# A transformer kernel that works out the second norm's sum of squares from sums taken with the output tiles

## The chip, the cores and the metric

One core of one Trainium2 chip runs the whole program. The time is device time in microseconds (us) from launch to end; the median of 3 runs of the kernel before is 2362.94 us (2359.41 to 2363.81).

## The reference

Two layers on 512 tokens of x and 256 tokens of ctx, 1024 channels (ctx is not needed after the first layer's feed-forward part), then one layer of another kind (dilated and neighbourhood attention, a router and experts), which starts with a norm as well. What matters here is how two norms follow one another. Cut to that:

```python
def rmsnorm(x, g):
    xf = x.astype(jnp.float32)
    y = xf * lax.rsqrt(jnp.mean(xf * xf, axis=-1, keepdims=True) + NORM_EPS)
    return (y * g.astype(jnp.float32)).astype(x.dtype)

for i in range(2):
    hx = rmsnorm(x, g_pre_mix[i]) * (1.0 + sc1) + sh1
    ...                                        # attention, Fourier, Hyena
    mix_x = jnp.concatenate([attn_x, four_x, hy_x], axis=-1) @ w_out[i]
    x = x + ga1 * rmsnorm(mix_x, g_post_mix[i])
    ...                                        # the same for ctx in layer 0
    fx = rmsnorm(x, g_pre_ffn[i]) * (1.0 + sc2) + sh2
    yx = conv_ffn(fx, w_up[i], w_ffn_conv[i], b_ffn_conv[i], w_down[i])
    x = x + ga2 * rmsnorm(yx, g_post_ffn[i])
```

So at four places a "post" norm of a product y (postmix and postffn in both layers) is followed at once by a "pre" norm of the new x. With G the gate times the gain, r1 and r2 the two 1/rms: x' = x + G r1 y, and the sum of x'^2 over the channels is sum x^2 + 2 r1 sum(G x y) + r1^2 sum(G^2 y^2).

## The kernel before

**Layout.** Channels lie on the 128 partitions and tokens on the free axis: x is 8 chunks (KT = 8) of 128 x 768 (512 of x, 256 of ctx; `W = T = 768` in layer 0, `TX = 512` from the feed-forward or mix output of layer 1 on). Every fp32 product is three passes of a split into a high and a low part (`hhi`/`hlo` for the activations, `whi`/`wlo` for the weights). Weights come as slabs of 128 x 1024 through a ring of three: SyncE issues the DMA into `wraw` in a fixed order (`ring_order`, L93), ScalarE rounds to `whi` (`split` L1497, `split_in` L1505), GpSimd subtracts for `wlo` (L649), TensorE uses the slab. Semaphores alone order the engines; each engine's list of instructions is written by hand.

**Sums over channels** are sums over partitions, so they go through TensorE. For the post norm ScalarE squares each output tile (L1826, L1876), VectorE adds the squares of tiles 0 to 6 into `yacc` (`add_squares` L2046), and `sums` (L805) multiplies `yacc` and the last square by a column of ones, one small product for each 128 tokens (each an fp32 product that appears as two instructions). `rms` (L1512) takes the square root, `inverse_rms` (L2034) the reciprocal and diagonal matrices `rdiag`, and `spread` (L842) multiplies them by ones, so that 1/rms stands in PSUM banks 6 and 7 (`rbc`) for every partition.

**Post norm and residual.** `post_norm` (L2079): VectorE multiplies y by gate and r1 (L2090, "gated" below), GpSimd adds chunks 0 to 4 to x (L655), VectorE chunks 5 to 7 (L2084).

**Pre norm.** In three of the four places ScalarE squares the new x as its chunks get ready (`norm_stats`, L1521), TensorE sums the squares over channels (`square` L818, L822), the row of sums is copied and turned (L1525, `turn_squares` L826), then again square root, reciprocal, `rdiag`, `spread`; then VectorE multiplies x by r2 (`norm_dve`, L2064), ScalarE applies gain and shift twice (`norm_apply`, L1557 full precision, L1559 rounded), VectorE subtracts for `hlo` (L2073). The first two tiles of the next product are interleaved over the chunks (`first_tiles` L758, L774), so that TensorE starts with chunk 0. At the fourth place, ahead of the last layer, the product runs on x not normed (`unnormed` L1536, `unnormed_low` L2460), and r2 multiplies the results (L2479); its sums of squares lie between the tiles (`square` as `behind`, `late_rms`).

**The feed-forward part** runs twice over 11 pairs of tiles (`CHUNKS = 2`, a hardware loop): 22 up tiles, then 8 down tiles (`down` L781), whose results VectorE adds to `y` (L2451). In layer 0 VectorE works meanwhile through 48 "column" slabs of the modulation weights (`mod_columns_of_c` L2400, L2413): they share the ring `wraw`, nine of them in the down tiles of each turn (one for each of tiles 0 to 6, two for tile 7). Column q lies in the ring behind down slab q+2, and a slot is fetched again only once its item is used (`after` L560), so the fetch of down slab q+4 waits for column q: column 6 lets down slab 10 come, column 7 the first slab of the next turn.

Of the kernel before, what the change touches and what calls it, by code (L numbers as in the profile page):

```python
# [29 lines left out]
P = 128  # L30
# [106 lines left out]
SUMS = 504  # L137
XT_BANK = (5, 1)
# [18 lines left out]
def program(nc, dram, out):  # L157
# [44 lines left out]
    rcol = sb("rcol", [P, T // P], place(T // P * 4))  # L202
    goh = sb("goh", [P, TX // P, NGRP], place(64))
# [15 lines left out]
    nsq = sb("nsq", [P, 2, T], ACT_O)  # L219
# [3 lines left out]
    nrow = sb("nrow", [P, 256], ACT_O + 7 * T * 4)  # L223
    up = sb("up", [P, 2, 2, T], SCR)
    ysq = sb("ysq", [P, 2, T], SCR)
    yacc = sb("yacc", [P, T], SCR + 2 * T * 4)
    sil = sb("sil", [P, T], SCR + 4 * T * 4)
# [125 lines left out]
    def pool_adds(key):  # L353

        return KT if key == (DEPTH - 1, "postffn") else 5

    def added(key, k):

        n = post_nth(key)
        return (sem("x_ready"), 5 * n + k + 1) if k < pool_adds(key) else (sem("x_late"), 3 * n + k - 4)  # L360
# [4 lines left out]

    def token_parts(width):


        w = 256 if width == T else P
        return w, [c * w % width for c in range(4)]  # L370

    def sq_nth(key):
        return pre_nth(key) - 1
# [262 lines left out]
    def _(pool):  # L636
# [9 lines left out]
        for n in range(N_SLABS):  # L646
# [4 lines left out]
            if n in add_after:  # L651
                key, W = add_after[n]
                for k in range(pool_adds(key)):
                    pool.wait_ge(sem("y_gated"), KT * post_nth(key) + k + 1)
                    pool.tensor_tensor(x[:, k, 0:W], x[:, k, 0:W], y[:, k, 0:W], ALU.add).then_inc(sem("x_ready"), 1)  # L655
                if key[1] == "postmix":
                    pool.wait_ge(sem("x_late"), 3 * post_nth(key) + 3)
# [57 lines left out]
    def _(pe):  # L715
# [97 lines left out]
        def squares(key, width):  # L813
            for k in range(KT):
                square(key, width, k, 2)
            turn_squares(key, width)

        def square(key, width, k, bank):  # L818
            w, parts = token_parts(width)
            pe.wait_ge(sem("sq_ready"), (KT + 1) * sq_nth(key) + k + 1)  # L820
            for c, t0 in enumerate(parts):
                m = pe.matmul(ps[32 * c:32 * c + 32, bank, 0:w], ones[:, 0:32], nsq[:, k % 2, t0:t0 + w],  # L822
                              start=k == 0, stop=k == KT - 1)
            m.then_inc(sem("sq_used"), 1)

        def turn_squares(key, width):  # L826
            w, _ = token_parts(width)
            pe.wait_ge(sem("sq_ready"), (KT + 1) * sq_nth(key) + KT + 1)
            for tt in range(width // P):
# [2125 lines left out]
```

## Time and profile before

| | |
|---|---|
| median of 3 runs | 2362.94 us |
| span of the profiled execution | 2360.5 us (its own time is not given apart; the median of the runs is 2.4 us above the span) |
| TensorE busy | 2202.1 us, 93% |
| VectorE busy | 1483.4 us, 63% |
| ScalarE busy | 1049.6 us, 44% |
| GpSimd busy | 663.2 us, 28% |
| mean granted TensorE clock | 0.964 of full speed |

The page of the profile gives busy time by engine, the span in 40 slices, the chain of work that ended last and the costliest groups of instructions. Further views are the chain in order of time, the timeline of one engine, groups of instructions by line, and the busy time and granted clock of chosen stretches. Where four short dips of TensorE stand in the 40 slices (0.8 to 0.9 of the clock at about 450, 1060, 1370 and 1760 us) the four pairs of norms lie.

### The profile page before, as it was taken

To read this page: it belongs to the slowest core of one execution; us is meant where nothing else is said; L and a number is where in the kernel's file an instruction comes from. 1 tells how busy PE (TensorE), PEld (TensorE's weight loads), DVE (VectorE), ACT (ScalarE), POOL (GpSimd) and SP (SyncE) were. 2 spreads that over 40 slices of the span, in tenths; PEclk is the share of its full clock that TensorE was granted. 3 is DMA by queue.
4 is the path that set the end of the run, shared out by engine and by line. 5 is a ranking of instruction groups with operands and counts; after the bars stand their busy time and mean duration, and the time that the engine had idled before them with its cause. 6 is when DMAs were issued, how large, how long until landed. Compare 5 with 4: busy or idle time off the path is not lost.

```text
span 2360.5 us, 31518 instructions
## 1 busy us (share of the span) xinstructions
PE 2202.1 (93%) x11722; PEld 1740.2 (74%) x11722; DVE 1483.4 (63%) x2656; ACT 1049.6 (44%) x1562; POOL 663.2 (28%) x298
## 2 busy tenths in 40 slices
PE   5999999799998999978999989999989998989997
PEld 2776668588887888866657768888868865777776
DVE  3565853478865787676676455435433269279998
ACT  3423852443322323225356354334332278357775
POOL 1221012322322223232300344444444410223223
PEclk8999999799999999978999979999989999989999
DMA  7431022123323233222410113223213221369996
GB/s 260 174 107 46 37 81 91 57 72 118 123 95 113 90 108 130 99 90 95 141 54 1 54 54 98 99 98 98 98 63 107 91 71 48 119 241 398 346 345 264
DMA packets 81901, 287.57 MB, mean 122 GB/s; under 512 B 10809, under 2 KB 13274, under 8 KB 80924
## 3 DMA queue, kind: packets, MB, share of 16 engines
q1 hardware_dynamic: 74768, 258.73, 31.5%
q10 hardware_dynamic: 3820, 13.24, 1.6%
q0 software_dynamic: 3168, 13.68, 1.5%
q8 instruction: 90, 1.47, 0.3%
q14 instruction: 55, 0.45, 0.1%
HBM read 279.83 MB, written 9.48 MB: 123 GB/s over the span
## 4 chain that ended last, share of the span: by engine, by line
PE 70%; DVE 16%; ACT 4%; issue 3%; DMA 2%; DVEq 2%; POOL 2%; SPq 0%; ACTq 0%
PE ps L729 31%; PE ps L798 11%; DVE mlo L2699 4%; PE ps L774 4%; DVE ps L2413 4%; PE ps L1462 2%; PE ps L1080 2%; PE ps L1096 2%; PE ps L1033 2%; PE ps L1322 2%; PE ps L1480 2%; DMA wraw<-in_w_all 1%; PE ps L1051 1%; POOL x L655 1%; PE ps L1137 1%
## 5 line engine op out<-in xcount | busy, mean ns | idle before, releaser
L649 POOL TENSOR_TENSOR wlo<-wraw,whi 128x1024 fp32r<-128x1024 f32 x208 | 505.1, 2431 | 1098.5 <-ACT whi L1510 637.9
L729 PE MATMUL ps<-hhi,whi 128*128 128x512 f32 (+1 forms) x1568 | 569.5, 363 | 6.2 <-POOL wlo L649 5.2
L729 PE MATMUL ps<-hlo,whi 128*128 128x512 f32 (+1 forms) x1568 | 563.0, 359 | 0.0
L729 PE MATMUL ps<-hhi,wlo 128*128 128x512 f32 (+1 forms) x1568 | 560.2, 357 | 0.0
L729 PEld LDWEIGHTS ps<-hhi,whi 128*128 128x128 f32 x1568 | 295.5, 188 | 74.4 <-issue 22.6
L729 PEld LDWEIGHTS ps<-hhi,wlo 128*128 128x128 f32 x1568 | 294.6, 188 | 45.9
L729 PEld LDWEIGHTS ps<-hlo,whi 128*128 128x128 f32 x1568 | 295.4, 188 | 43.9 <-issue 1.0
L1510 ACT ACTIVATE whi<-wraw 128x1024 fp32r<-128x1024 f32 x132 | 139.1, 1054 | 308.0 <-DMA wraw<-in_w_all 229.7
L2413 DVE CUSTOM_DVE_ANT_0 ps<-wraw,crow,mod 128x256 f32<-128x256 f32 x384 | 224.4, 645 | 18.1 <-issue 11.7
L2699 DVE TENSOR_TENSOR mlo<-mraw,mhi 128x1024 fp32r<-128x1024 f32 x147 | 207.1, 1439 | 5.1 <-ACT mhi L1964 5.0
L798 PE MATMUL ps<-alo,whi 128*128 128x512 f32 (+1 forms) x528 | 187.9, 356 | 0.0
L798 PE MATMUL ps<-ahi,whi 128*128 128x512 f32 (+1 forms) x528 | 187.6, 355 | 0.3 <-POOL wlo L649 0.2
L798 PE MATMUL ps<-ahi,wlo 128*128 128x512 f32 (+1 forms) x528 | 186.6, 353 | 0.0
L1964 ACT ACTIVATE mhi<-mraw 128x1024 fp32r<-128x1024 f32 x168 | 168.1, 1051 | 6.4 <-DMA mraw<-in_w_moe 6.0
L2105 DVE SCALAR_TENSOR_TENSOR up<-ps,cconv,up 128x511 f32<-128x511 f32 (+1 forms) x132 | 83.1, 658 | 129.3 <-ACT up L1852 126.4
L1503 ACT ACTIVATE whi<-wraw 128x1024 fp32r<-128x1024 f32 x76 | 80.3, 1058 | 106.0 <-PE ps L729 86.8
L1852 ACT ACTIVATE up<-ps,cconv 128x768 f32<-128x768 f32 (+1 forms) x88 | 77.3, 879 | 104.5 <-PE ps L729 104.0
L691 POOL TENSOR_TENSOR mlo<-mraw,mhi 128x1024 fp32r<-128x1024 f32 x21 | 67.4, 3208 | 169.8 <-ACT mhi L1964 169.8
L798 PEld LDWEIGHTS ps<-ahi,whi 128*128 128x128 f32 x528 | 99.6, 189 | 15.7 <-POOL wlo L649 0.7
L2451 DVE TENSOR_TENSOR y<-y,ps 128x768 f32<-128x768 f32 (+1 forms) x32 | 26.2, 820 | 134.3 <-PE ps L798 134.3
L798 PEld LDWEIGHTS ps<-ahi,wlo 128*128 128x128 f32 x528 | 99.2, 188 | 14.7
L798 PEld LDWEIGHTS ps<-alo,whi 128*128 128x128 f32 x528 | 99.5, 188 | 13.9
(368 smaller groups left out, 3835.6 us busy)
## 6 DMA issues: line engine op xcount, KB each, us to landing
wraw<-in_w_all SPq DMA_DIRECT2D x288, 512.0 KB, 3.5
mraw<-in_w_moe SPq DMA_DIRECT2D x168, 512.0 KB, 6.2
mraw_b<-in_w_mod SPq DMA_DIRECT2D x10, 512.0 KB, 15.4
fl<-in_four ACTq DMA_DIRECT2D x2, 2048.0 KB, 8.1
slot_rows<-in_slot_rows ACTq DMA_DIRECT2D x1, 3612.0 KB, 21.5
xs<-slot_rows POOLq DMA_DIRECT2D x7, 516.0 KB, 7.6
mraw_a<-in_w_mod SPq DMA_DIRECT2D x6, 512.0 KB, 10.8
x<-in_xT SPq DMA_DIRECT2D x1, 2048.0 KB, 9.4
```

The lines of the kernel that those rows point to most:

```text
L649: pool.tensor_tensor(wlo[:, slot, :], wraw[:, AT_W[n] % RING, :], whi[:, slot, :].bitcast(F32), ALU.subtract).then_inc(lo_split, 1)
L691: pool.tensor_tensor(mlo2[:, n % MS, :], mraw2[:, n % MR, :], mhi2[:, n % MS, :].bitcast(F32), ALU.subtract).then_inc(pool_lo, 1)
L729: m = pe.matmul(ps[:, bank + b, 0:w], a, r[:, c0:c0 + w], start=k == 0 and q == 0, stop=k == KT - 1 and q == 2)
L774: m = pe.matmul(ps[:, bank + b, 0:w], a, r[:, c0:c0 + w], start=k == 0 and q == 0, stop=k == KT - 1 and q == 2)
L798: m = pe.matmul(ps[:, bank + b, 0:w], a, r[:, c0:c0 + w], start=k == 0 and z == 0, stop=k == PAIRS - 1 and z == 2)
L1503: act.activation(whi[:, n % RING, :], wraw[:, AT_W[n] % RING, :], ACT.Copy).then_inc(hi_split, 1)
L1510: act.activation(whi[:, n % RING, :], wraw[:, AT_W[n] % RING, :], ACT.Copy).then_inc(hi_split, 1)
L1852: act.activation(up[:, p % 2, z, 0:W], psf[:, b * 512:b * 512 + W], ACT.Identity, bias=cconv[:, s, 3:4], scale=cconv[:, s, 1:2]).then_inc( ...
L1964: act.activation(mhi2[:, m % MS, :], mraw2[:, n % MR, :], ACT.Copy).then_inc(ring_hi, 1)
L2105: dve.scalar_tensor_tensor(dst[:, c0 + 1:c0 + w], ps[:, bank + b, 0:w - 1], w0, dst[:, c0 + 1:c0 + w], ALU.mult, ALU.add)
L2413: m = dve.tensor_tensor_reduce(ps[:, 6 + j % 2, s * COL_W:(s + 1) * COL_W], slab[:, j, :], crow[:, s, :], 1.0, modf[:, c:c + 1], ALU.mult, ...
L2699: dve.tensor_tensor(mlo2[:, m % MS, :], mraw2[:, n % MR, :], mhi2[:, m % MS, :].bitcast(F32), ALU.subtract).then_inc(ring_lo, 1)
```

## The change

The sum of squares of the new x is no longer taken from the new x. While the output tiles come, VectorE adds up two more rows of 128 x W: `gacc` = sum of G^2 y^2 (from the squares that are there) and `xacc` = sum of G x y (a product x*y into SBUF, or PSUM in the down tiles, then a multiply-add). `cross_sums` sums both over channels on TensorE behind `summed_squares`, `pair_stats` puts the formula together in five small operations and makes both `rdiag`s, `paired_rms` on ScalarE takes the second root; `norm_pair` then runs the gated products, GpSimd's additions (now all 8 chunks), the products with r2 (from two other PSUM banks) and the `hlo` subtractions interleaved. All `squares`, `turn_squares`, `norm_stats`, `nsq`, `nrow` are gone, in the fourth place too; there the first tile that may run behind the first two waits for `r_kept`, and ScalarE splits two weight slabs only after that. ScalarE also takes the ctx part of the full-precision gain and shift (was L2069 on VectorE). `gains(L, 3)` of layer 0 moves ahead of the down tiles. The core of the diff:

```diff
@@ gpsimd
-                for k in range(pool_adds(key)):
+                for k in range(KT):
                     pool.wait_ge(sem("y_gated"), KT * post_nth(key) + k + 1)
                     pool.tensor_tensor(x[:, k, 0:W], x[:, k, 0:W], y[:, k, 0:W], ALU.add).then_inc(sem("x_ready"), 1)
@@ tensor
+        def cross_sums(key, width, t):
+            pe.wait_ge(acc_free, t)
+            pe.wait_ge(sem("xsum_ready"), post_nth(key) + 1)
+            for c, src in zip(CROSS, (xacc, gacc)):
+                for tt in range(width // P):
+                    m = pe.matmul(ps[:, bank2(t - 1) + 1, c + tt:c + tt + 1], src[:, tt * P:tt * P + P], ones[:, 0:1],
+                                  start=True, stop=True)
+            m.then_inc(sem("xsum_used"), 1)
...
+        def norm_pair(post, width, stage, t):
+            summed_squares(post, width, stage)
+            cross_sums(post, width, t)
+            spread(post, width, 6, rdiag)
+            spread(following(post), width, bank2(t - 1), rdiag2)
...
-            summed_squares((L, "postmix"), W, mix_nth(L))
-            spread((L, "postmix"), W)
-            squares((L, "preffn"), W)
-            spread((L, "preffn"), W)
+            norm_pair((L, "postmix"), W, mix_nth(L), T0 + IN_T + OUT_T)
...
-        first_tiles(B2_SLAB, B2_TILE, B2_SLAB, B2_TILE, h_rhs, [TX, TX], False,
-                    sem("h_ready"), KT * pre_nth((2, "premix")), None, lambda k: square((2, "premix"), TX, k, 3))
+        first_tiles(B2_SLAB, B2_TILE, B2_SLAB, B2_TILE, h_rhs, [TX, TX], False,
+                    sem("h_ready"), KT * pre_nth((2, "premix")))
         for s in range(2, IN2_T):
+            if s == 2:
+                pe.wait_ge(sem("r_kept"), 1)
@@ scalar
+        def paired_rms(post, width):
+            key = following(post)
+            act.wait_ge(sem("scol_ready"), post_nth(post) + 1)
+            act.activation(rcol2[:, 0:width // P], scol[:, 0, 0:width // P], ACT.Sqrt, bias=eps_c, scale=1.0 / D)\
+               .then_inc(sem("std_ready"), 1)
@@ norm_apply
                 act.activation(nfull[:, k % 2, 0:TX], nt[:, k % 2, 0:TX], ACT.Identity, bias=bfn(k, 0), scale=afn(k, 0))
+                if width == T and key != norms[0]:
+                    act.activation(nfull[:, k % 2, TX:T], nt[:, k % 2, TX:T], ACT.Identity, bias=bfn(k, 1), scale=afn(k, 1))
@@ vector
+        def add_cross(k, L, gate, width, tmp):
+            for c0, w, b in segs[width]:
+                a, q = gacc[:, c0:c0 + w], ysq[:, k % 2, c0:c0 + w]
+                if k == 0:
+                    m = dve.tensor_scalar(a, q, g2[:, k, b:b + 1], None, ALU.mult)
+                else:
+                    m = dve.scalar_tensor_tensor(a, q, g2[:, k, b:b + 1], a, ALU.mult, ALU.add)
+            if k < KT - 1:
+                m.then_inc(sem("ysq_used"), 1)
+            dve.tensor_tensor(tmp, y[:, k, 0:width], x[:, k, 0:width], ALU.mult)
+            dve.drain()
+            for c0, w, b in segs[width]:
+                a, q = xacc[:, c0:c0 + w], tmp[:, c0:c0 + w]
+                if k == 0:
+                    m = dve.tensor_scalar(a, q, mv[:, L, gate, k, b:b + 1], None, ALU.mult)
+                else:
+                    m = dve.scalar_tensor_tensor(a, q, mv[:, L, gate, k, b:b + 1], a, ALU.mult, ALU.add)
+            dve.drain()
+            if k == KT - 1:
+                m.then_inc(sem("xsum_ready"), 1)
...
+        def pair_stats(post, width, t1):
+            inverse_rms(post, width, rcol, rdiag)
+            ...                       # five operations of 128 x 4 or 6, a drain behind each
+            dve.tensor_scalar(total, total, 0.0, None, ALU.max).then_inc(sem("scol_ready"), 1)
+            inverse_rms(following(post), width, rcol2, rdiag2)
+            dve.wait_ge(sem("r_ready"), nth(post) + 1)
...
+        def norm_pair(post, L, gate, width, t):
+            pair_stats(post, width, t)
+            ...
+            for k in range(KT + 3):
+                if k < KT:
+                    gated(post, L, gate, width, k)
+                if 2 <= k < KT + 2:
+                    q = k - 2
+                    if q == 0:
+                        dve.wait_ge(sem("r_ready"), nth(pre) + 1)
+                    dve.wait_ge(sem("x_ready"), KT * post_nth(post) + q + 1)
+                    if q >= 2:
+                        dve.wait_ge(sem("full_ready"), before + q - 1)
+                    dve.tensor_tensor(nt[:, q % 2, 0:width], x[:, q, 0:width], r2, ALU.mult)\
+                       .then_inc(sem("scaled_ready"), 1)
+                if k >= 3:
+                    q = k - 3
+                    dve.wait_ge(sem("full_ready"), before + q + 1)
+                    dve.tensor_tensor(hlo[:, q, 0:width], nfull[:, q % 2, 0:width], hhi[:, q, 0:width].bitcast(F32),
+                                      ALU.subtract).then_inc(sem("h_ready"), 1)
@@ output tiles of the mix
-            for s in range(OUT_T - 1):
-                add_squares(s, KT * mix_nth(L), W)
+            for s in range(OUT_T):
+                if s < OUT_T - 1:
+                    add_squares(s, KT * mix_nth(L), W)
+                else:
+                    dve.drain().then_inc(sem("ysum_ready"), 1)
+                    dve.wait_ge(sem("ysq_ready"), KT * mix_nth(L) + KT)
+                dve.wait_ge(acc_free, T0 + IN_T + s + 1)
+                add_cross(s, L, 1, W, xy[:, 0:W])
@@ down tiles
+                tmp = psf[:, 3072:3072 + W]
                 for o in range(KT):
...
                     dve.tensor_tensor(y[:, o, 0:W], y[:, o, 0:W], psf[:, b * 512:b * 512 + W], ALU.add)\
                        .then_inc(acc_free, 1)
                     if o:
+                        dve.drain()
                         add_squares(o - 1, i * KT + KT * ffn_nth(L), W)
+                        add_cross(o - 1, L, 3, W, tmp)
             dve.drain().then_inc(sem("ysum_ready"), 1)
+            dve.wait_ge(sem("ysq_ready"), KT * (ffn_nth(L) + CHUNKS))
+            add_cross(KT - 1, L, 3, W, xy[:, 0:W])
```

## Rows read from the trace of the kernel before

**Rows 1.** The page: busy time by engine.

```profile
PE 2202.1 (93%) x11722; PEld 1740.2 (74%) x11722; DVE 1483.4 (63%) x2656; ACT 1049.6 (44%) x1562; POOL 663.2 (28%) x298
```

**Rows 2.** The chain in order of time, layer 0, postmix to preffn: start, us, what.

```profile
434.76 2.59 PE ps L809 x24
438.55 2.94 PE ps L851 x6
441.51 1.15 DVE y L2090 x2
466.35 19.59 PE ps L774 x96
```

**Rows 3.** Stretches: busy by engine (PE first), then PEclk, the granted clock.

```profile
440.00:442.00 2.00, 1.47 (x5) 0.75 (x3) 0.49 (x1) 0.00 (x0) 1.16 (x1) 0.50 0.00 0
240.00:245.00 5.00, 3.29 (x27) 2.56 (x27) 3.10 (x7) 3.55 (x7) 0.00 (x0) 1.00 0.00 0
```

**Rows 4.** Groups by shape between the tiles, 434.7 to 485.8 us: busy us, mean ns.

```profile
L655 POOL TENSOR_TENSOR x<-x,y 128x768 f32<-128x768 f32 x5 | 9.6, 1965 | 1.6 <-DVE y L2090 1.6
L2064 DVE TENSOR_TENSOR nt<-x,ps 128x768 f32<-128x768 f32 x8 | 7.5, 948 | 2.6 <-PE ps L851 2.6
L1557 ACT ACTIVATE nfull<-nt,mod,mv 128x512 f32<-128x512 f32 x8 | 6.5, 814 | 5.9 <-DVE nt L2064 5.9
L1559 ACT ACTIVATE hhi<-nt,mod,mv 128x256 fp32r<-128x256 f32 x8 | 4.7, 587 | 0.0
L2084 DVE TENSOR_TENSOR x<-x,y 128x768 f32<-128x768 f32 x3 | 3.9, 1313 | 0.2
```

**Rows 5.** Timeline of VectorE: layer 0's last two down tiles of both turns, with idle before.

```profile
736.69 0.95 DVE L2451 TENSOR_TENSOR y<-y,ps 128x768 f32<-128x768 f32 x1 [4.02 <-PE ps L798]
738.27 2.52 DVE L2052 TENSOR_TENSOR yacc<-yacc,ysq 128x768 f32<-128x768 f32 x1 [0.63 <-ACT ysq L1876]
1036.52 0.95 DVE L2451 TENSOR_TENSOR y<-y,ps 128x768 f32<-128x768 f32 x1 [0.16 <-PE ps L798]
1040.75 4.75 DVE L2136 SCALAR_TENSOR_TENSOR mv<-mod,vec 128x8 f32<-128x8 f32 x8 [0.37 <-issue]
```

**Rows 6.** Timelines of ScalarE and GpSimd, layer 0, ends of mix and second turn.

```profile
435.50 0.81 ACT L1828 ACTIVATE y<-ps 128x768 f32<-128x768 f32 x1
438.66 2.50 POOL L649 TENSOR_TENSOR wlo<-wraw,whi 128x1024 fp32r<-128x1024 f32 x1 [7.75 <-ACT whi L1503]
...
1040.42 4.66 POOL L649 TENSOR_TENSOR wlo<-wraw,whi 128x1024 fp32r<-128x1024 f32 x2 [0.85 <-ACT whi L1510]
```

**Rows 7.** The chain in order of time, from the first to the second turn of layer 0.

```profile
744.75 3.60 DMA wraw<-in_w_all
755.17 18.66 PE ps L774 x96
```

**Rows 8.** The chain in order of time, layer 0 postffn to layer 1 premix.

```profile
1040.71 5.29 PE ps L809 x24
1050.17 1.15 DVE y L2090 x2
1090.59 0.97 DVE hlo L2073
```

**Rows 9.** The chain in order of time, layer 1, postmix to preffn.

```profile
1357.46 1.75 PE ps L809 x16
1362.38 0.76 DVE y L2090
1363.21 6.66 POOL x L655 x5
1381.24 13.71 PE ps L774 x48
```

**Rows 10.** The chain in order of time, layer 1 postffn to the last layer.

```profile
1751.19 0.76 DVE y L2090
1781.41 5.75 PE ps L729 x24
```

More of the change, by code:

```diff
@@ L351, in post_nth, with following @@
         return [k for k in norms if k[1][:4] == "post"].index(key)
[L353 to L360, printed above, removed]
+    def following(key):
+        return norms[norms.index(key) + 1]
     def sum_nth(key):
         return 0 if key == norms[0] else 1 + post_nth(key)
[L366 to L373, printed above, removed]
     def mix_nth(L):
@@ L811, in sums @@
             return m
[L813 to L829, printed above, removed]
-                c, t0 = tt * P // w, tt * P % w
-                m = pe.matmul(ps[:, 7, SUMS + tt:SUMS + tt + 1], nrow[:, t0:t0 + P], ident[:, 32 * c:32 * c + 1],
-                              start=True, stop=True)
-            m.then_inc(sem("sq_used"), 1)
         def summed_squares(key, width, stage):
@@ L840, in summed_squares, with spread @@
             sums(ysq[:, (KT - 1) % 2, :], width, False, True).then_inc(sem("ysum_used"), 1)
-        def spread(key, width):
-            rd = rdiag[:, :, :].rearrange("p t n -> p (t n)")
+        def cross_sums(key, width, t):
[6 more added lines that the diff above has]
+            m.then_inc(sem("xsum_used"), 1)
+        def spread(key, width, bank, diag):
+            rd = diag[:, :, :].rearrange("p t n -> p (t n)")
             half = width // 2
@@ L893, in _ @@
         mod_turn(1, MOD_BANK[1])
-        spread((0, "premix"), T)
+        spread((0, "premix"), T, 6, rdiag)
         def late_mods(k):
@@ L911, in _ @@
             S0, T0 = L * LAYER_SLABS, L * LAYER_TILES
-            if L:
-                squares((L, "premix"), T)
-                spread((L, "premix"), T)
             first_tiles(S0, T0, S0, T0, h_rhs, [in_width(L, 0), in_width(L, 1)], L == 0,
@@ L1534, in summed_rms, with unnormed @@
             rms(key, width)
-        def unnormed(key, width, ready, before, gain, bank):
+        def unnormed(width, ready, before, gain):
             for k in range(KT):
@@ new lines, in gated @@
+        def gated(key, L, gate, width, k):
+            for c0, w, b in segs[width]:
+                m = dve.scalar_tensor_tensor(y[:, k, c0:c0 + w], y[:, k, c0:c0 + w], mv[:, L, gate, k, b:b + 1],
+                                             rbc[:, c0:c0 + w], ALU.mult, ALU.mult)
+            m.then_inc(sem("y_gated"), 1)
+        def norm_pair(post, L, gate, width, t):
+            pair_stats(post, width, t)
+            pre = following(post)
+            r2 = psf[:, bank2(t - 1) * 512:bank2(t - 1) * 512 + width]
+            before = KT * pre_nth(pre)
+            for k in range(KT + 3):
+                if k < KT:
+                    gated(post, L, gate, width, k)
[13 more added lines that the diff above has]
+                                      ALU.subtract).then_inc(sem("h_ready"), 1)
@@ L2441, in _ @@
                 dve.wait_ge(sem("y_clear"), L + 1)
+                if L == 0:
+                    gains(L, 3)
+                gate_squares(L, 3)
+                tmp = psf[:, 3072:3072 + W]
                 for o in range(KT):
@@ L2464, in unnormed_low @@
                    .then_inc(sem("h_ready"), 1)
-            post_norm((L, "postffn"), L, 3, W, unnormed_low if L else None)
+            if L == 0:
+                norm_pair((L, "postffn"), L, 3, W, T0 + LAYER_TILES)
+            else:
+                pair_stats((L, "postffn"), W, T0 + LAYER_TILES)
+                for k in range(KT + 3):
+                    if k < KT:
+                        gated((L, "postffn"), L, 3, W, k)
+                    if k >= 3:
+                        unnormed_low(k - 3)
         def qk_low(s):
```

123 lines of the change are left out of this document (49 added, 74 removed).

## The prediction

> **What bounds the kernel now.** I read the page first: TensorE is busy 93% of the span, the others far less [rows 1], so a change pays only where TensorE waits. Then I went through the chain in order of time around the four pairs of norms. In layer 0 the last output tile ends at 434.76, the post norm's sums and spread lead to the first gated product at 441.51, and the first tile of the next product starts only at 466.35 [rows 2]: 31.6 us without a tile, of which 24.8 lie between gated product and tile. The same distance is 18.9 us in layer 1 (1362.38 to 1381.24) [rows 9]. The chain inside it is addition on GpSimd, square, sum, root, spread: that is what the change takes out. Two more things matter. Behind the first pair TensorE works off eight chunks for 19.59 us [rows 2], so an earlier start helps only as far as chunks come fast enough. And in layer 0's down tiles VectorE is nearly full: the y addition of tile 6 still waits 4.02 us for TensorE, that of the last tile only 0.16 [rows 5], and the DMA that column 7 sets free (744.75, 3.60 us) lies on the chain to the start of the second turn at 755.17 [rows 7].
>
> **The added work on VectorE, per tile.** `add_cross` is two multiply-adds over the two segments (1.15 us for such a pair [rows 2]) and one product of 128x768 (0.95 [rows 4]): with drains 3.3 us in layer 0 and, at two thirds of the width, 2.2 in layer 1. Under the mix output tiles this is hidden (a tile is some 9.6 us, VectorE adds one square in it). Without that cover each tile would cost its 3.3. It is not hidden in two places.
>
> First, the columns. The sums over tile 4 stand ahead of column 6, those over tile 5 ahead of column 7. Column 6 frees slab 10, whose split ScalarE does before the square of tile 5, which VectorE needs before column 7: the chain has no slack from column 6 on. Of the first 3.3 us I take 2.3, because the wait for GpSimd that column 6 had now falls partly on the sums; the second 3.3 counts whole. Column 7 is 5.6 us late (bounds 3.3 and 6.6, all hidden and nothing hidden in the first), and so are the first slab of the next turn and the start at 755.17: **+5.6 us**.
>
> Second, the ends of the four stages, where the last sums stand ahead of everything, below.
>
> **The port that VectorE and GpSimd share.** Tiny `gains` products of 128x8 last 4.75 us for eight [rows 5] while GpSimd runs two subtractions, 4.66 us [rows 6]; VectorE's addition x+y takes 1.31 on average beside GpSimd's additions, a product of the same size with one PSUM operand 0.95 [rows 4]. So VectorE operations with two SBUF operands wait for a running GpSimd operation. The new loop puts `hlo` subtractions with two SBUF operands right beside GpSimd's eight additions. The rule that speaks against this change is in the Trainium skill, "SBUF — State Buffer", section "SBUF: two separate sides": the pair is an exclusive lock, and whoever comes second waits for the whole instruction. By it the pace below is 3.8 us a chunk; were it a mere slowing like the 0.36 us on L2084, the pace would be 3.2 and each layer 0 pair 3 us cheaper.
>
> **Pace of the new loop**, from the first gated product at 0 (layer 0): gated 1.06 each (1.15 for the pair, less overlap), GpSimd 1.8 (9.6 us for five with some waiting), product with r2 0.87, ScalarE 0.81+0.59 twice, less overlap 2.4, subtraction 0.9 [rows 4]. Chunk 0: third gated product ends at 3.2, r2 product 4.2, ScalarE 6.7, the subtraction waits for GpSimd's fourth addition until 8.3: ready at 9.3. Then per chunk gated 1.06, GpSimd 1.8 (the r2 product runs beside it), subtraction 0.9: 3.8. Ready times 9.3, 13.1, 16.9, 20.7, 24.5; once the gated products are through, ScalarE's 2.4 sets 26.3, 28.8, 31.2. TensorE needs 4 us a chunk at the half clock and 2.1 at the full one; the last chunk ends at **33.3**. In layer 1 the parts are 0.67, 1.3, 0.62, 1.5 and 0.65: ready from 6.5 to 21.2, end **22.6**. Before, the ends lay at 44.4 (485.94 less 441.51) and 32.6 (1394.95 less 1362.38). So 11 and 10 us are won from the first gated product on.
>
> **What stands ahead of the gated product.** TensorE sums two more rows: 24 instructions in layer 0, 16 in layer 1. The old 24 took 2.59 at the full clock [rows 2] and 5.29 at the low one [rows 8]. The granted clock after the last tile is 0.50, the 1.2 GHz level [rows 3], and TensorE will have stood still longer than before: I take 5.3 and 3.5 (bounds 2.6 and 5.3; 1.8 and 3.5). Behind them `spread`, 2.94, and as VectorE makes the second `rdiag` before it looks at r1, 0.2 more (0.6 in layer 1, where the spread is only 2.1). The second root, reciprocal and spread lie behind the first three gated products and cost nothing; without those they would cost 3 us.
>
> *Pair 1 (layer 0, mix).* The y copy ends at 436.3 [rows 6]; sums 3.3; the GpSimd subtraction that starts at 438.66 gets in between the last two products, so +2.5: 442.2. Sums on TensorE 447.5, spread and rest 450.65, against 441.51. End 483.95 against 485.94: **−2.0** (from −9 with no blocking, to +6 if the clock stays low).
>
> *Pair 2 (layer 0, feed-forward).* The sums on TensorE started at 1040.71. Now: 5.6 late by column 7, 3.3 for tile 6, whose sums stand ahead of the signal, and 4.66 blocked by two GpSimd subtractions: 1054.3. The old 24 sums 1059.6, the new ones 1064.9 (VectorE is ready at 1057.6), rest 3.15: first gated product at 1068.05 against 1050.17. Last chunk ready at 31.2 on: 1099.25 against 1091.56 (1090.59 + 0.97) [rows 8], from where ScalarE's DMA issues and the next tile follow as before: **+7.7** (+3 without blocking).
>
> *Pair 3 (layer 1, mix).* Last tile 1357.46, copy 1.1, sums 2.2, TensorE 3.5, rest 2.7: 1367.0 against 1362.38; end 1389.6 against 1394.95: **−5.3** (−9 to 0).
>
> *Pair 4.* The 1/rms of x was never waited for here. The gated product comes some 7.5 us later than 1751.19 by the same steps. Given back: the squares between the first tiles, the turned row and spread inside the third tile and its wait for r2; the fourth tile started at 1781.41, 30.2 us behind the gated product [rows 10]. Without those some 22.4 remain (first chunk at 4.0 as before, then 1.7 a chunk by GpSimd's additions, 16.4 in all, third tile 6.0): 1781.1. **0** (−2 to +3). The slabs split later are first needed a tile later.
>
> In layer 1's down tiles (7.5 us each, no columns) 2.2 us are hidden.
>
> **Sum:** −2.0 + 5.6 + 7.7 − 5.3 + 0 = +6.0 us. The span of 2360.5 becomes 2366.5; the profiled execution's own time is not given apart, the median of the runs lies 2.4 us above the span, so 2369.
>
> **Rivals.**
> *1, faster: the port is no matter and column 6 hides the sums.* Pair 1 then starts at 448.05 and ends 28.8 on (−9.1), the turn costs +3.3, pair 2 −3.8, pair 3 −8.7, pair 4 −0.5: −18.8, 2344. For it: the additions in GpSimd's five show little blocking (1.965 mean). Against it: 4.75 us for eight tiny products. Chance 0.17.
> *2, no change: the new sums run at the full clock.* 2.7 less in pairs 1 and 2, 1.8 in pair 3: −7.2, so 2362. Against it: 0.50 in [rows 3]. Chance 0.18.
> *3, much slower: the clock.* TensorE takes chunks of 2.1 us every 3.8. If such gaps keep it at 1.2 GHz, it needs 4 us a chunk and 2.6 in layer 1, the ends come at 40.9 and 27.3: pair 1 +5.6, pair 2 +10, pair 3 −0.6, pair 4 +2, the turn 5.6: +22.7, 2386. Decisive is whether work of 55% holds the full clock once it is there. Against it: a stretch with TensorE busy 3.29 of 5 us stays at 1.00 [rows 3]. Chance 0.15.
> *4, the change doesn't do what it says:* the first tile still waits for the second root. Then pairs 1 and 3 win nothing and the added sums stay, some +25, 2388. In the order of the instructions nothing of the kind stands: below 0.01, counted with rival 3.
>
> **How the numbers follow.** My case has 0.50 and its own range is 2364 to 2374. With 0.17 at 2344 and 0.15 at 2386, 8 in 10 reach from 2353 to 2384. A measurement of this kernel tells some 0.2%, 4.7 us, from no change: faster, below 2358.2, is rival 1 and a part of rival 2: 0.23; same is most of rival 2 and the low edge of mine: 0.24; slower 0.53.
>
> **What will show it.** In the trace after: first gated products near 450.7, some 1073.7 (1068.05 + 5.6), and so on with the shifts; from gated product to first tile 9.5 us instead of 24.8 in layer 0; `hlo` subtractions of 1.5 to 2 us while GpSimd adds; the gap ahead of the second turn 5 to 6 us later in layer 0; TensorE's 24 new instructions in 5.3 us. I am wrong if the subtractions keep 0.96 us, if column 7 is less than 3 us late, or if the clock in the first two tiles stays at 0.50 to their end.

## The result and the profile after

The changed kernel takes 2374.11 us (median of 4, 2373.09 to 2376.27) against 2362.89 for the kernel before: ratio 1.0055, 95% interval 1.0043 to 1.0068, so 11.2 us slower. I had forecast 2369, 6 us slower, with a range of its own from 2364 to 2374: the measured time lies at its upper edge. Its profiled span is 2371.6 us, 11.1 above that of before. The page first, TensorE to GpSimd, to be held against [rows 1]:

```profile
PE 2194.8 (93%) x11506; PEld 1748.4 (74%) x11506; DVE 1628.3 (69%) x2844; ACT 1034.5 (44%) x1542; POOL 679.9 (29%) x307
```

VectorE has 145 us more to do, TensorE 7 us less: the price lies in what TensorE waits for, and in a lower granted clock behind some of these waits. The chain of the first pair (start, us, what; before in [rows 2]):

```profile
438.90 0.75 DVE xacc L2029
439.66 2.49 DVEq L2030
...
442.28 5.27 PE ps L816 x24
...
450.37 3.06 DVE y L2087 x6
```

The new sums end, wait 2.49 us for a GpSimd subtraction, and TensorE's 24 new instructions take 5.27 us. The first gated product starts at 450.34, where I had 450.65; the first tile starts 9.3 us later, at 459.64, and TensorE is through with the first tiles at 483.67, where before it was at 485.78. How fast the chunks come is in the groups by shape of VectorE between 450 and 485 us (count, busy us, mean ns, idle before):

```profile
L2112 DVE TENSOR_TENSOR hlo<-nfull,hhi 128x768 fp32r<-128x768 f32 x8 | 13.1, 1640 | 2.9 <-ACT hhi L1518 2.9
L2107 DVE TENSOR_TENSOR nt<-x,ps 128x768 f32<-128x768 f32 x8 | 7.6, 944 | 0.0
```

The subtraction with two SBUF operands takes 1640 ns in the mean (1.94 us beside an addition), the product with one PSUM operand 944. The stretches (busy of PE, PEld, DVE, ACT, POOL, then the granted clock) show 0.50, the 1.2 GHz level, for the row sums, and 1.00 from 470 to 480, although TensorE is busy only 7.71 of 10 us there:

```profile
440.00:447.00 7.00, 4.72 (x23) 4.75 (x23) 3.35 (x4) 0.00 (x0) 1.85 (x1) 0.50 0.23 77
470.00:480.00 10.00, 7.71 (x41) 6.42 (x42) 8.18 (x9) 8.50 (x15) 7.09 (x3) 1.00 0.00 1
```

The second turn of layer 0 starts later. This is TensorE's timeline at that place, with the idle time ahead (before: 755.17 [rows 7]):

```profile
758.23 0.80 PE L764 MATMUL ps<-hhi,whi 128*128 128x512 f32 x1 [10.10 <-POOL wlo L640]
```

The chain of the second pair answers to [rows 8]; there the old sums started at 1040.71 and the first gated product at 1050.17:

```profile
1051.07 2.47 DVE yacc L2009
...
1054.19 2.49 DVE gacc L2019
1056.68 3.02 DVE ps L2022
...
1061.22 5.28 PE ps L799 x24
1066.50 5.13 PE ps L816 x24
...
1074.45 3.06 DVE y L2087 x6
```

Three additions and products that take 0.95 to 1.15 us alone take 2.47, 3.22 and 3.10 us in VectorE's timeline, while GpSimd runs three subtractions (1050.38, then two in 5.31 us from 1053.57). The first of the three took 2.47 us in the kernel before, too. In layer 1, where before the sums ran at 1357.46 and the gated product at 1362.38 [rows 9], the chain shows what I had not foreseen, VectorE behind its tiles:

```profile
1358.20 2.80 DVE xy L2022
...
1363.94 2.73 DVE xacc L2029
...
1368.77 2.90 DVE xacc L2029
...
1377.38 3.56 PE ps L816 x16
```

Ledger of the two traces, each mark less the same mark before, in steps. The marks are the ends of the first tiles behind each pair and TensorE's start of the second turn; where the next instruction starts at once, its start stands for the end:

| place | before | after | step | forecast |
|---|---|---|---|---|
| pair 1, next tile | 485.78 | 483.67 | -2.1 | -2.0 |
| second turn of layer 0 | 755.17 | 758.23 | +5.2 | +5.6 |
| pair 2, first tiles done | 1094.28 | 1108.20 | +10.9 | +7.7 |
| pair 3, next tile | 1394.79 | 1405.05 | -3.7 | -5.3 |
| to the end | 2360.5 | 2371.6 | +0.8 | 0 |

A profile is one execution. The first sums of pair 1, up to which all kernels but a few operations agree, start between 433.3 and 437.8 in the traces of this study; so below distances between two marks of one trace are compared, not times of day, and one of 1 or 2 us proves little by itself.

### The profile page after: what moved, and what is told of

The parts are those of the page before. It is cut to its first block, busy times and chain, and to the rows that moved or that the text cites. A ratio compares the mean times of both kernels' runs of the same rounds, so it can differ in the third digit from the quotient of the medians.

```text
span 2371.6 us, 31352 instructions
## 1 busy us (share of the span) xinstructions
PE 2194.8 (93%) x11506; PEld 1748.4 (74%) x11506; DVE 1628.3 (69%) x2844; ACT 1034.5 (44%) x1542; POOL 679.9 (29%) x307
## 4 chain that ended last, share of the span: by engine, by line
PE 65%; DVE 21%; ACT 4%; issue 3%; DVEq 2%; DMA 2%; POOL 1%; SPq 0%; ACTq 0%
PE ps L719 30%; PE ps L788 11%; DVE mlo L2734 5%; DVE ps L2434 5%; PE ps L764 3%; PE ps L1062 2%; PE ps L1078 2%; PE ps L1015 2%; PE ps L1295 2%; PE ps L1033 1%; PE ps L1119 1%; PE ps L1435 1%; PE ps L1453 1%; PE ps L844 1%; DVE hlo L2112 1%
## 5 line engine op out<-in xcount | busy, mean ns | idle before, releaser
L719 PE MATMUL ps<-hhi,whi 128*128 128x512 f32 (+1 forms) x1568 | 570.5, 364 | 5.9 <-POOL wlo L640 5.9
L764 PE MATMUL ps<-hhi,whi 128*128 128x512 f32 (+1 forms) x168 | 69.4, 413 | 52.8 <-DVE hlo L2112 29.1
L788 PEld LDWEIGHTS ps<-ahi,wlo 128*128 128x128 f32 x528 | 99.7, 189 | 14.8
## 6 DMA issues: line engine op xcount, KB each, us to landing
mraw_b<-in_w_mod SPq DMA_DIRECT2D x10, 512.0 KB, 15.4
```

Of the source, the lines that this page charges most:

```text
L719: m = pe.matmul(ps[:, bank + b, 0:w], a, r[:, c0:c0 + w], start=k == 0 and q == 0, stop=k == KT - 1 and q == 2)
L764: m = pe.matmul(ps[:, bank + b, 0:w], a, r[:, c0:c0 + w], start=k == 0 and q == 0, stop=k == KT - 1 and q == 2)
L788: m = pe.matmul(ps[:, bank + b, 0:w], a, r[:, c0:c0 + w], start=k == 0 and z == 0, stop=k == PAIRS - 1 and z == 2)
```

## Experiments: the sums under the down tiles

In the changed kernel the first of the two feed-forward turns takes its sums for nothing: the second starts them anew. To leave them out there, it must first be written out; that alone is the base.

```diff
-            with dve.Fori(0, CHUNKS) as i:
+            for i in range(CHUNKS):
```

> The changed kernel with VectorE's loop over the two feed-forward turns written out twice instead of a counted loop; every instruction and wait is the same. It is the base for the run in which only the last turn takes its sums. Theory: the loop itself costs nothing that TensorE waits for, 2374 us as the changed kernel (2372 to 2376). Rival: the doubled code, which has to be loaded, delays VectorE by some us at each turn of layer 0, where it has little slack (the wait for TensorE ahead of the y addition of tile 7 is 0.16 us): 2377 or more.

Measured: 2373.8 us, ratio 1.0045 (1.0030 to 1.0061). The written-out loop costs nothing that the times show.

The next run takes the sums only in the second turn (the gains for them, too, which the cut leaves out):

```diff
-                        add_squares(o - 1, i * KT + KT * ffn_nth(L), W)
-                        add_cross(o - 1, L, 3, W, tmp)
+                        m = add_squares(o - 1, i * KT + KT * ffn_nth(L), W)
+                        if i == CHUNKS - 1:
+                            add_cross(o - 1, L, 3, W, tmp)
+                        else:
+                            m.then_inc(sem("ysq_used"), 1)
...
```

> As the kernel with the loop written out, but the sums (and the gains and squared gains they need) are taken with the down tiles of the second turn only; those of the first turn are thrown away in the changed kernel anyway. Theory (the sums of tiles 4 and 5 push columns 6 and 7, and these the slabs of the next turn): the second turn of layer 0 starts where it did before, less the 2.1 us of pair 1, 5.2 us earlier than in the changed kernel; all of it is kept: 2374.1 - 5.2 = 2369 us. Rival (the start of the second turn hangs on DMAs alone, or what is won there is lost in the second turn, whose columns are the bottleneck): at most 1.5 us, 2373.

Measured: 2369.5 us, 1.0025 (1.0013 to 1.0038), 4.3 us less than its base. From the tile behind pair 1 to the second turn it needs 268.8 us (486.51 to 755.35), its base 274.8, the kernel before 269.4. TensorE's timeline at the turn, the base and this run:

```profile
757.48 0.80 PE L764 MATMUL ps<-hhi,whi 128*128 128x512 f32 x1 [8.53 <-POOL wlo L640]
```

```profile
755.35 0.79 PE L764 MATMUL ps<-hhi,whi 128*128 128x512 f32 x1 [6.53 <-POOL wlo L640]
```

So the chain of columns, transfer and split is shown for the first turn. Of the 6.0 us in the traces the times keep 4.3, and the intervals of the two ratios overlap a little; TensorE also stands still longer at the second turn of layer 1 (2.70 us against 1.47, see under `gated_psum`). The next run leaves the sums out in both turns of both layers, but for the last tile of each stage, so its second statistic covers one tile of eight.

```diff
-                        add_squares(o - 1, i * KT + KT * ffn_nth(L), W)
-                        add_cross(o - 1, L, 3, W, tmp)
+                        add_squares(o - 1, i * KT + KT * ffn_nth(L), W).then_inc(sem("ysq_used"), 1)
...
-            add_cross(KT - 1, L, 3, W, xy[:, 0:W])
+            add_cross(KT - 1, L, 3, W, xy[:, 0:W], True)
```

> The changed kernel without the sums of the down tiles but for the last one of each stage, in both layers (so the second statistic behind the feed-forward stages covers one tile of eight). Theory: the sums under the tiles of layer 0 are what pair 2 and the turn cost. The turn comes 5.2 us earlier; in the second turn the columns are on time, and the row sums start near 1044 less 5 instead of 1061.2, but the sums of the last tile still wait for one GpSimd subtraction: pair 2 gives back 13 to 15 us of the 17.4 by which the row sums are later than before. 2374.1 - 5.2 - 14 = 2355 us. Rival (hidden sums; what costs is the serial part behind the last tile: its products, 24 more row sums, the spread): 2374.1 - 5 = 2369.

Measured: 2356.2 us, 0.9972 (0.9961 to 0.9983), 17.9 less than the changed kernel and below the kernel before. The row sums of pair 2 start at 1040.77 instead of 1061.22; the new ones, ready 1.27 us behind the old, cost little (TensorE's timeline, idle in brackets):

```profile
1040.77 2.72 PE L799 MATMUL ps<-ones,yacc 128*128 128x1 f32 x12 [4.18 <-DVEq L2482]
1043.35 2.70 PE L799 MATMUL ps<-ones,ysq 128*128 128x1 f32 x12
1047.32 0.34 PE L816 MATMUL ps<-ones,xacc 128*128 128x1 f32 x1 [1.27 <-DVE xacc L2027]
```

The sums under the feed-forward tiles are thus the whole loss and more: with one tile's sums of eight the change would win 6.6 us.

The same cut made in a kernel that computes everything: new pairs behind the mix, old ones behind the feed-forward stages.

```diff
-            norm_pair((L, "postffn"), W, ffn_nth(L) + CHUNKS - 1, T0 + LAYER_TILES)
+            summed_squares((L, "postffn"), W, ffn_nth(L) + CHUNKS - 1)
+            spread((L, "postffn"), W, 6, rdiag)
```

> Only the pairs behind the mix are the new ones (sums with the output tiles, both 1/rms together); behind the feed-forward stages the sums of the down tiles are gone, and the squares of x, their sums and the second root are as before. Theory, from the ledger of the two traces: pair 1 gives 2.1 us and pair 3 some 3.6, the turn and pairs 2 and 4 cost nothing: 2362.9 - 5.7 = 2357 us. Rival (the pairs lean on each other: pair 1's win is lost to the DMA chain ahead of the second turn, since transfers and not TensorE set its start): 2360 or more.

Measured: 2359.3 us, 0.9985 (0.9976 to 0.9994): 3.5 us faster than before, 2 short of my theory. The rival is right that a part of pair 1's win is lost, but not ahead of the second turn: it goes in it. In its trace the second turn starts at 752.65, 2.5 us before that of the kernel before; its sums start at 1041.76, 1 us after. The waits of TensorE in the second turn, this kernel and the kernel before (us in total, times, longest):

```profile
PE ps L785 <- POOL wlo L661: 6.6, 1, 6.6
...
PE ps L740 <- POOL wlo L661: 3.0, 2, 1.9
PE ps L809 <- POOL wlo L661: 0.9, 1, 0.9
```

```profile
PE ps L774 <- POOL wlo L649: 6.5, 1, 6.5
...
PE ps L729 <- POOL wlo L649: 1.7, 1, 1.7
```

2.3 us more are spent waiting for split slabs. The three traces that leave out the sums under the down tiles, all or all but the last (this one, the one above and the last below) start the turn at 751.6 to 753.6, the kernel before at 755.2, and all four have their row sums at 1040.7 to 1041.8: an earlier turn is not an earlier end. In `no_down` the granted clock also falls to 0.50 for a stretch behind such a wait (1.77 us, at 891.10). What sets that moment, transfers or columns, I did not separate.

## Experiments: the port

```diff
-  pool.tensor_tensor(x[:, k, 0:W], x[:, k, 0:W], y[:, k, 0:W], ALU.add)
+  pool.tensor_tensor(x[:, k, 0:8], x[:, k, 0:8], y[:, k, 0:8], ALU.add)
```

> The changed kernel with GpSimd adding only 8 columns of y to x in each of its additions (the rest of x stays without y). Theory (the lock): with nothing of length on GpSimd the hlo subtractions take 0.9 us instead of 1.94 in layer 0, 0.65 instead of 1.39 in layer 1; the pace falls from 3.8 to 2.9 us a chunk and then to ScalarE's 2.4: 4.5 us less in each of the two pairs before full-width tiles, 4 behind the mix of layer 1, 1 in the last: 2374.1 - 14 = 2360 us. Rival (the subtraction is slow by itself): the hlo subtraction keeps 1.9 us and the time is 2372 or more.

Measured: 2361.5 us, 0.9997 (0.9986 to 1.0009), 12.6 less than the changed kernel. VectorE between 450 and 485 us:

```profile
L2112 DVE TENSOR_TENSOR hlo<-nfull,hhi 128x768 fp32r<-128x768 f32 x8 | 7.6, 954 | 3.5 <-ACT hhi L1518 3.5
```

From the gated product to the next tile are 28.5 us instead of 33.3 in pair 1, 29.0 instead of 33.8 in pair 2. Here the work was taken from GpSimd; the next run leaves it and moves an operand, behind the mix of layer 1 alone.

```diff
-   act.activation(nfull[:, k % 2, 0:TX], nt[:, k % 2, 0:TX], ACT.Identity, bias=bfn(k, 0), scale=afn(k, 0))
+   act.activation(full_of(key, k, TX), nt[:, k % 2, 0:TX], ACT.Identity, bias=bfn(k, 0), scale=afn(k, 0))
...
+    def full_of(key, k, w):
+        if key == (1, "preffn"):
+            c = (bank2(LAYER_TILES + IN_T + OUT_T + k % 2) + 1) * 512
+            return psf[:, c:c + w]
+        return nfull[:, k % 2, 0:w]
```

> The changed kernel with one operand of the hlo subtraction (the full-precision h) written to PSUM instead of SBUF, behind the mix of layer 1 alone, where PSUM has room. Theory (two-SBUF operations of VectorE wait for a running addition of GpSimd): the subtraction falls from 1.39 us to about 0.65, the pace from 2.57 to 1.95 us a chunk, the first tiles end 4 to 5 us earlier: 2374.1 - 4.5 = 2369.6 us. Rival (the subtraction is long because it waits for ScalarE or because of its own operands): it keeps over 1.2 us, 2374.

Measured: 2369.8 us, 1.0039 (1.0025 to 1.0053), where 2369.6 stood. The subtraction in the changed kernel (1380 to 1406 us) and in this one:

```profile
L2112 DVE TENSOR_TENSOR hlo<-nfull,hhi 128x512 fp32r<-128x512 f32 x8 | 8.7, 1086 | 1.5 <-ACT hhi L1518 1.5
```

```profile
L2118 DVE TENSOR_TENSOR hlo<-ps,hhi 128x512 fp32r<-128x512 f32 x8 | 5.5, 686 | 1.6 <-ACT hhi L1524 1.5
```

The same subtraction beside the same additions takes 686 ns once one input lies in PSUM, and the tile follows the gated product by 18.7 us instead of 21.7. The two runs show from two sides that VectorE's subtraction with both inputs in SBUF waits for GpSimd's additions. A result in PSUM does not help: in the chain of the second pair the product x*y, two inputs in SBUF and its result in PSUM, took 3.10 us. This is the lock of the Trainium skill's "SBUF — State Buffer", section "SBUF: two separate sides", against a mere slowing, as I had weighed it.

## Experiments: the row sums and the order

```diff
-            for c, src in zip(CROSS, (xacc, gacc)):
+            for c, src in zip(CROSS[:1], (xacc,)):
```

> The changed kernel without the row sums of one of the two new rows (12 of the 24 instructions in layer 0, 8 of 16 in layer 1; the second statistic takes the other row's sum for it). Theory (they run at 1.2 GHz, 0.22 us each, and nothing runs beside them): 2.65 + 2.6 + 1.75 + 1.7 = 8.7 us less, 2365.4 us. Rival (the first root, reciprocal and the diagonal take as long, or what is won is lost to GpSimd's subtraction or the clock): at most 3, 2371 or more.

Measured: 2364.8 us, 1.0010 (0.9997 to 1.0024), 9.3 less. From the old sums to the first gated product it is 12.8 us instead of 15.4 in pair 1 and 10.7 instead of 13.2 in pair 2, so each of the 12 instructions costs its 0.22 us. Behind the mix of layer 1 nothing was won (298.4 us from pair 2's end to pair 3's, 296.9 in the changed kernel): the old row sums took 3.58 us there at a granted clock of 0.50, in the changed kernel 1.94 at 0.98. From there to the end of pair 4's first tiles it needs 379.6 us instead of 382.7; 1.1 of these is a pause of TensorE that this run lacks (see under `gated_psum`), so that the total agrees with the forecast partly by luck.

If the row sums stand in the way, put them behind the gated products:

```diff
             summed_squares(post, width, stage)
-            cross_sums(post, width, t)
             spread(post, width, 6, rdiag)
+            cross_sums(post, width, t)
...
+            for k in range(5):
+                gated(post, L, gate, width, k)
+            pair_stats(post, width, t)
```

> The changed kernel with another order behind the sums: TensorE spreads the first 1/rms before it takes the two new row sums, and VectorE makes five gated products before it looks at the second statistic, the other three around its root, and then the eight products with r2 and the eight subtractions. Behind the last stage the second root and spread lie beside the first tiles. Theory (the new row sums, 5.3 us in layer 0 and 3.5 in layer 1, stand ahead of everything, and the pace of 3.8 us a chunk is VectorE's): first gated product 4.7 us earlier in layer 0; r2 comes 2.5 us later than now, but with the gated products and most additions behind it the chunks then come every 2.4 us (ScalarE), so that the last of them is ready 3 to 4 us earlier; 2.5 earlier behind the mix of layer 1, 3 at the last stage: 2374.1 - 13 = 2361 us. Rival (the chunks hang on r2, which comes later): +2 in three pairs, -3 in the last, 2377.

Measured: 2383.6 us, 1.0095 (1.0081 to 1.0109): 9.4 us slower than the changed kernel; my theory fell. The chain of pair 1:

```profile
453.77 0.16 DVE scol L2085
...
454.00 0.86 DVE scol L2087
...
454.94 1.68 DVE scol L2089
...
456.70 1.69 DVE scol L2091
...
459.60 2.13 DVE rdiag L2007
...
461.77 2.94 PE ps L829 x6
```

Operations on 128x6 numbers take up to 1.69 us: they now run beside GpSimd's additions, and those with all operands in SBUF each wait for the end of one. The first two, which read a sum from PSUM, keep 0.16. Next, their results in PSUM:

```diff
-            r1, total, t = rcol[:, 0:n], scol[:, 0, 0:n], scol[:, 1, 0:n]
+            r1, total, t, u = rcol[:, 0:n], scol[:, 0, 0:n], ps[:, bank, 464:464 + n], ps[:, bank, 472:472 + n]
...
-            dve.tensor_scalar(total, total, 0.0, None, ALU.max).then_inc(sem("scol_ready"), 1)
+            dve.tensor_scalar(u, t, 0.0, None, ALU.max).then_inc(sem("scol_ready"), 1)
```

> The run with the gated products first, with VectorE's small operations on the second statistic writing to PSUM (each has one SBUF operand or none; sum, root and reciprocal stay there, the diagonal is a product of SBUF with PSUM). In the run before three of the five 128x6 operations took 0.86, 1.68 and 1.69 us beside GpSimd's additions and the diagonal 2.6 instead of 1.0. Theory (even a tiny operation waits for a whole addition if its operands lie in SBUF): they take 0.2 us each, r2 comes 5.6 us earlier in layer 0 and 3 to 4 in layer 1: 2383.6 - 18 = 2366 us, so below the changed kernel by 8. Rival (the new order loses by TensorE's clock, low until the first tile, and the row sums that come later; the small operations are beside the point): 2378 or more.

Measured: 2373.4 us, 1.0051 (1.0038 to 1.0064), 10.2 less than the run before, not 18. The small operations do as the theory says (VectorE's timeline):

```profile
452.08 0.17 DVE L2093 TENSOR_TENSOR ps<-ps,rcol 128x6 f32<-128x6 f32 x1
452.32 0.17 DVE L2095 TENSOR_TENSOR ps<-scol,ps 128x6 f32<-128x6 f32 x1
452.57 0.17 DVE L2097 TENSOR_SCALAR ps<-ps 128x6 f32<-128x6 f32 x1
```

The old sums to the next tile now are 46.0 us in pair 1 and 45.2 in pair 2, against 51.4 and 50.3 in the run before and 48.7 and 47.0 in the changed kernel: 5.4 and 5.1 us a pair, where 5.6 was computed. Behind the mix of layer 1 it is 30.4 against 30.1 in the changed kernel, no gain, and from there to the sums of the last stage it needs 3.5 us more than the changed kernel (359.3 against 355.7). The 3.5 us have a cause in TensorE's timeline. At the start of layer 1's second feed-forward turn it stands still for 2.75 us, and the profile names nothing it waits for (`last_turn`, `no_down`, `no_l1_mix` and `gated_first` 2.7 to 2.8, changed kernel 1.10, kernel before none):

```profile
1574.76 0.54 PE L767 MATMUL ps<-hhi,wlo 128*128 128x512 f32 x1 [2.75 <-issue]
```

That is 1.6 us more than in the changed kernel, and behind it the granted clock falls: from 1576 to 1580 us it is 0.72, with 14 instructions, against 1.00 and 17 in the changed kernel. All nine kernels with a pause there (1.07 to 2.76 us), and `half_sums` without one, show one packet of the DMA queue for instructions within 2 us of the turn's start; the kernel before, `mix_only` and `mix_psum` show none. Code that arrives late would fit, but no run changes that alone. The missing 8 us are another matter, as `gated_first` has the same pause. Its profiled run was the slowest of its five: between the two traces lie 14.8 us, of which the three pairs ahead of full-width tiles have 5.4, 5.1 and 4.4, between the medians only 10.2. Why the medians lie closer stays open.

## Experiments: the mix tiles of layer 1

```diff
+                if L and s < OUT_T - 1:
+                    add_squares(s, KT * mix_nth(L), W).then_inc(sem("ysq_used"), 1)
+                    continue
```

> The changed kernel without the new sums under the mix tiles of layer 1, but for the last tile (so the third of the four second statistics covers one tile of eight). Theory (a mix tile there lasts 5.44 us, VectorE needs some 5 for it with the sums and GpSimd's blocking, and carries a backlog out of the three early tiles: the sums start 2.9 us behind the last tile, the new row sums 5.4): the first go at once, the new ones at most 3.5 us behind the tile; with 0.7 us of the early tiles 2.5 us are given back, 2371.6. Rival (the last tile's own sums and their wait for GpSimd are what costs): 2374, the row sums of the new rows still 5 us behind the last tile.

Measured: 2371.3 us, 1.0041 (1.0026 to 1.0055), as forecast, though the interval reaches the changed kernel's. The trace is clearer: the first sums start at 1370.03, at once behind the last tile, the new ones 3.2 us later, and from pair 2's end to pair 3's it is 293.1 us instead of 296.9 (part of it is lost again to the pause of 2.7 us named above). The sums under these tiles thus cost 3.8 us.

Last, the kernel with new pairs behind the mix only, and in layer 1 whatever fits in PSUM: h in full precision, the squares of y (`sq_of`, banks 1 and 3), and x*y (bank 5).

```diff
-  act.activation(ysq[:, s % 2, 0:W], psf[:, b * 512:b * 512 + W], ACT.Square)
+  act.activation(sq_of(L, s, W), psf[:, b * 512:b * 512 + W], ACT.Square)
...
-  add_cross(s, L, 1, W, xy[:, 0:W])
+  add_cross(s, L, 1, W, psf[:, 2560:2560 + W] if L and s < OUT_T - 1 else xy[:, 0:W], sq_of(L, s, W))
```

> The run with the new pairs behind the mix only, and in layer 1 the operands in PSUM that there is room for: the full-precision h of the pair, the squares of y and the product x*y of the mix tiles but the last. Theory: 3.0 us from the subtraction (as in the run with that alone, where the first tiles took 18.7 us from the first gated product instead of 21.7), 2.5 from VectorE's backlog under the mix tiles: 2359.3 - 5.5 = 2354 us, 0.4% below the kernel before. Rival (the backlog stays, as the product y*x still waits for GpSimd): 2356.5.

Measured: 2351.6 us, 0.9960 (0.9946 to 0.9974): faster than both kernels, 9.6 us (0.4%) below the kernel before in the same runs (2361.1). The same pairs without it were 3.5 us below the kernel before in theirs (2362.8), so the operands in PSUM are worth some 6.0 us (5.5 forecast; the bare times differ by 7.7). The trace is that of the fastest of its six runs (2346.9 to 2355.8). VectorE's groups of the mix tiles (count, busy, mean ns), first the changed kernel, then this one:

```profile
L2022 DVE TENSOR_TENSOR xy<-y,x 128x512 f32<-128x512 f32 x8 | 9.9, 1235 | 0.0
L2029 DVE SCALAR_TENSOR_TENSOR xacc<-xy,mv,xacc 128x512 f32<-128x512 f32 x7 | 9.4, 1340 | 0.5
L2019 DVE SCALAR_TENSOR_TENSOR gacc<-ysq,g,gacc 128x512 f32<-128x512 f32 x7 | 7.4, 1051 | 0.2 <-issue 0.2
L2009 DVE TENSOR_TENSOR yacc<-yacc,ysq 128x512 f32<-128x512 f32 x6 | 6.2, 1034 | 0.5
```

```profile
L2109 DVE TENSOR_TENSOR ps<-y,x 128x512 f32<-128x512 f32 x7 | 4.8, 691 | 0.0
L2116 DVE SCALAR_TENSOR_TENSOR xacc<-ps,mv,xacc 128x512 f32<-128x512 f32 x6 | 4.5, 751 | 0.4
L2106 DVE SCALAR_TENSOR_TENSOR gacc<-ps,g,gacc 128x512 f32<-128x512 f32 x6 | 4.5, 745 | 0.0
L2096 DVE TENSOR_TENSOR yacc<-yacc,ps 128x512 f32<-128x512 f32 x6 | 4.1, 687 | 10.3 <-ACT ps L1871 10.2
```

The idle column tells it: no time between operations in the changed kernel, 10.3 us for six tiles here. The product x*y still has two SBUF inputs and yet takes 691 ns. The timelines of VectorE and GpSimd say why:

```profile
1344.95 0.69 DVE L2109 TENSOR_TENSOR ps<-y,x 128x512 f32<-128x512 f32 x1
1345.72 0.75 DVE L2116 SCALAR_TENSOR_TENSOR xacc<-ps,mv,xacc 128x512 f32<-128x512 f32 x1
```

```profile
1345.18 2.71 POOL L673 TENSOR_TENSOR wlo<-wraw,whi 128x1024 fp32r<-128x1024 f32 x1 [2.73 <-ACT whi L1539]
```

With VectorE on time the product starts 0.2 us ahead of the subtraction, and the operation behind it, which reads the product from PSUM, runs beside it in 0.75 us. In the changed kernel VectorE is late, so its SBUF operations fall under the subtraction, and as I read it that keeps it late; no run changes the lateness alone. From pair 2's end to pair 3's it is 288.4 us, against 300.5 before: 12.1 won, of which the changed kernel kept 3.7.

## Why the prediction was right in sign and half the size

- **What bounds the kernel, and pair 1:** right. Sums 5.27 us at half clock (5.3), gated product at 450.34 (450.65), first chunk 9.3 us behind it (9.3), 3.77 to 3.79 us a chunk (3.8), end -2.1 (-2.0). `half_sums` shows the sums on the path, `short_adds` and `psum_nfull` the port as the cause of the pace. That denies rival 1 (a harmless port); the granted clock denies rival 2 (sums at full clock) and rival 3 (a clock that stays low to the end of the first tiles).
- **Columns of the first turn:** right, +5.2 for +5.6, and 6.0 in the trace of `last_turn`.
- **Pair 2:** the mis-sized term is the delay of column 7 in the second turn, for which I took the 5.6 us of the first. The last y addition starts at 1049.38 against 1036.52 [rows 5]: 12.9 later, less 3.1 of the turn 9.8. VectorE's first y addition of the second turn, in the kernel before and in the changed one:

```profile
956.75 0.95 DVE L2451 TENSOR_TENSOR y<-y,ps 128x768 f32<-128x768 f32 x1
```

```profile
963.59 0.94 DVE L2476 TENSOR_TENSOR y<-y,ps 128x768 f32<-128x768 f32 x1
```

From the first y addition to the last it is 85.8 us against 79.8: 6.0, close to the 5.6, with one product x*y ahead of column 6 that waits for GpSimd (3.17 us at 1022.58). The other 3.8 are lost ahead of the first down tile, where no new sum stands (205.4 us from the start of the turn, 201.6 before), and my sum had no term for them. TensorE waits for split slabs 0.74 us at 878.77, where before it did not, and 2.13 at 897.97, where before it was 1.66. Behind the longer wait the granted clock falls, first the changed kernel, then the kernel before (busy of PE, PEld, DVE, ACT, POOL, then the granted clock):

```profile
896.00:904.00 8.00, 6.03 (x25) 5.19 (x26) 6.79 (x10) 4.10 (x6) 3.34 (x2) 0.79 0.43 164
```

```profile
891.00:899.00 8.00, 6.34 (x37) 5.38 (x36) 6.85 (x12) 3.98 (x6) 2.93 (x2) 1.00 0.42 161
```

Twelve instructions fewer in 8 us are some 2 us at the pace of the full clock (59 in 10 us), so this and the wait of 0.74 are most of the 3.8. From the last y addition on all fits: 11.8 us to the sums against 4.2 before (+7.7; I had 8.0), 13.2 from the sums to the gated product (13.75), 33.8 to the end.
- **Pair 3:** the step that failed is "under the mix output tiles this is hidden", which I worked out for layer 0 (tiles of 9.6 us) and let stand for layer 1. There a tile takes 5.44 us, VectorE's part with the blocking some 5 (2.9 by themselves and 2.1 blocked), so that it works off only 0.4 us a tile of what it is behind by the three early tiles. The row sums came 5.4 us behind the last tile. `no_l1_mix` and `mix_psum` show it. I had used the port for single operations at the ends and not for the stages between.
- **Pair 4:** +0.8 for 0. The gated product comes 19.1 us later than before, 11.6 of them before the last y addition: 7.5, as forecast. What was given back held too: the fourth tile starts at 1793.56 against 1781.41 [rows 10], 12.2 later. The +0.8 holds the 1.1 us pause at layer 1's second turn, which I did not foresee, so that the term came out this near partly by luck.

## What to carry to other kernels

Before work goes to VectorE "under" a stage, set its time per tile, with each SBUF-only operation lengthened by what GpSimd runs there, against the tile's time in every layer: near the tile's time a backlog is hardly worked off. Putting an input of such operations into PSUM (for the 128x6 ones the results with it) took the wait away each time it was tried; a result alone in PSUM did not. Work in a loop whose result only the last turn uses is paid in every turn: here 6.0 us in the traces, 4.3 in the times. And an engine that waits a little longer can lose its clock on top: price a longer wait of TensorE with the stretch at half clock that may follow it.

## What the runs showed of the hardware

- VectorE's 128x6 operations took 0.16 us alone and 0.86, 1.68 and 1.69 beside GpSimd's 1.8 us additions, the last a comparison of one SBUF operand with a constant; with input and result in PSUM it took 0.17.
- TensorE kept the granted clock of 1.00 over 10 us in which it was busy 7.71 (pair 1, chunks every 3.8 us), after 0.50 in the gap ahead.
- In the up tiles of layer 0's second turn TensorE waited once for 1.5 to 2.2 us. In five traces (waits of 1.77 and 2.09 to 2.18 us) its granted clock then fell to 0.50 for some 3 to 4 us; in the other eight (1.48 to 1.91) it stayed at 1.00. So the length of this wait alone did not decide it in these traces.
